# First FFN group's norm transposed on TensorE, its x tiles loaded together, mixer weight casts tied to the FFN's progress, weight ring in the gate/up region

## The chip, the cores and the metric

The kernel runs on all 8 cores of one Trainium2 chip. Each core takes two of the 16 sequences (4096 tokens) through the whole layer with its own copy of the weights; the cores exchange nothing. The time of a run is the device time of the slowest core in microseconds (us). Three runs of the kernel before gave 3274.52 to 3281.97 us, median 3280.74.

A core has five engines with one instruction queue each: TensorE (PE, matmuls; PEld is its weight load), VectorE (DVE), ScalarE (ACT), GpSimd (POOL) and SyncE (SP), which here issues DMAs only. An engine takes its queue in order, and an instruction that waits holds up all behind it. SP's and POOL's DMAs run on the same 16 DMA engines. SBUF (128 partitions) holds operands, PSUM has eight banks of 128x512 fp32 that matmuls write.

## The reference

One decoder layer, D = 1024, sequences of 2048:

```
x = x + 1/2 * SwiGLU_1(RMSNorm(x))                      # FFN1, d_ff = 2816
h = RMSNorm(x)
[q_lat | kv_lat | k_rope | xc | Bg | Cg | gate_logits] = h @ w_in
A: latent attention, 8 heads, QK-norm, rotary part, causal, softmax
B: y_B = Bg * conv3(Cg * xc)                            # causal depthwise, width 3
merged = sigmoid(gA) * (y_A @ w_proj_attn) + sigmoid(gB) * (y_B @ w_proj_conv)
x = x + merged @ w_out
x = x + 1/2 * SwiGLU_2(RMSNorm(x))                      # FFN2
swiglu(h) = (silu(h @ w_gate) * (h @ w_up)) @ w_down
```

x and the weights arrive as float32; the kernel's matmuls are bf16 with fp32 sums.

## The kernel before, in words

**Tiles and stages.** The 4096 tokens are 8 groups of 512 (NG, G), a group is four tiles of 128 (TPG). Three stages follow each other: FFN1 over all groups, the mixer (attention and convolution), FFN2. Sums between the stages go through DRAM (x1s, x2s). The FFN's inner width is 22 chunks of 128 (NFC).

**The norm** (`norm_stream`, L833) runs per tile: a load of x into one of two buffers (xin, L841), a square with a running sum on ACT (L860), two small POOL operations for 1/rms (L862, L864), one DVE operation that scales and rounds to bf16 (xn, L866), and a DMA transpose (L869) that writes hT, the group's activations with the features on the partitions. hT has two buffers for even and odd groups. The loads run one tile ahead.

**FFN1** (`ffn_stream`, L874): for each of 22 chunks, 8 matmuls for gate and 8 for up against hT (their issue is the helper's line L708), SiLU on ACT (L906), product on DVE (L908, aact). Then w_down. In the first group the loop over chunks kc is the outer one there, over all eight PSUM banks, so that it can follow the loading of w_down; x is added and stored to x1s (L937, L941).

**Weights.** FFN1's come as fp32 and are rounded on the core (`load_w1`, L779): gate/up pieces of 128x2048 through five staging buffers (astg, L783), rounded by ACT (L786) and DVE (L788) into agu; w_down in pieces of 128x1024 (L795) through four buffers (axr twice and dscr twice), rounded by ACT (L798) and DVE (L800) into awd. The weights of the mixer and of FFN2 are rounded from DRAM to DRAM (wms) by casting DMAs of POOL (`cast_w`, L820 and L830). `cast_w` waits for flags of FFN1's progress (`f1.1.0`, `f1.1.7`, ...), but a flag says that the planner has placed that work, not that the chip has done it.

**The ring.** In the mixer the convolution's, gate's and projections' weights pass through ten buffers of 128x1024 bf16 (`ring_stream`, L1186, in `use_order`). Its stream begins once FFN1 has been placed to its end.

**What sets the order.** Each stream above is a generator of operations. A planner (`FW.schedule`) takes at each step the operation with the earliest estimated start over all streams, with costs for each operation and rates for DMAs (DMA_RATE bytes per ns for SP, SWDMA_RATE for POOL), and appends it to its engine's queue with the semaphore waits that its buffers need. Among near equals the stream that stands first in the list goes first. So the order within every queue is fixed when the program is built; on the chip only the waits act.

**SBUF.** After the permanent buffers one region is laid out three times: for FFN1 (gate/up weights, sg, act, w_down, xr), for the mixer, and for FFN2. A buffer may be written once the work that used its addresses before has been placed, and the write waits on the chip for that work's semaphores. In the mixer's layout V and K of a whole sequence come one after the other, and the ring stands last, over FFN1's and FFN2's w_down and xr.

**The gated merge** (`proj`): per chunk of 128 features four products, gate A, gate B, conv (8 matmuls) and attention (4 matmuls), in three PSUM banks in turn; DVE reads the last two (L1319, L1321).

Of the kernel before, what the change touches and what calls it, by code (L numbers as in the profile page):

```python
# [177 lines left out]
class Op:  # L178
    __slots__ = ("eng", "fns", "reads", "writes", "cost", "sem", "nbytes")

    def __init__(self, eng, fns, reads, writes, cost, sem=None, nbytes=0):
# [6 lines left out]
        self.nbytes = nbytes  # L188

# [13 lines left out]
DMA_RATE = 340.0  # L203
# [3 lines left out]
class FW:  # L207
# [20 lines left out]
    def deps_of(self, op, commit):  # L228
# [17 lines left out]
        for group, is_w in ((op.reads, False), (op.writes, True)):  # L246
            for d in group:
# [220 lines left out]
def build_program():  # L468
# [19 lines left out]
    cst_d = nc.dram_tensor("cst", [128, 128], F32, kind="ExternalInput").ap()  # L488
# [81 lines left out]
    def ffn_bufs(tag):  # L570
# [30 lines left out]
    f1 = ffn_bufs("a")  # L601
    for b in f1.all:
# [14 lines left out]

    wlat = mb("wlat", [8, LATW], BF16)
# [13 lines left out]
    QT = [mb(f"QT{i}", [NH, G], BF16) for i in range(2)]  # L632
    d_QT = []
    for q_ in QT:
        dl = [Dep(f"QT.{t}") for t in range(TPG)]
        for dp in dl:
            dp.anc = list(q_.d[0].anc)
        q_.new = [(q_.addr, q_.end, dp) for dp in dl]
        q_.d = dl
        d_QT.append(dl)  # L640
    NKT = S // 128
    Vc = mb("Vc", [NKT, 4, 192], BF16, NKT)
    d_V = Vc.d
    NPT = 3
    KT = mb("KT", [NKT, NH, 128], BF16, NKT)
# [4 lines left out]
    M_END = a  # L650
# [46 lines left out]
    s_set = [fw.new_dma_sem(f"set{i}") for i in range(4)]  # L697
# [4 lines left out]
    def dma(eng, sem, fn, reads, writes, nbytes):  # L702
        return Op(eng, fn, reads, writes, 330.0 if eng == "sp" else 600.0, sem, nbytes)
# [73 lines left out]
    def load_w1():  # L777
        yield Wait(lambda: "seta" in flags)
        for c in range(NFC):  # L779
            yield Wait(lambda c=c: c < 2 or f"f1.t.0.{min(c - 2, TPG - 1)}" in flags)  # L780
# [8 lines left out]
                     [sb.d[1]], [gu.d[1]], c_dve(1024, 2))  # L789
        yield Do(lambda: flags.add("f1.stg"))  # L790
        yield Wait(lambda: "rope" in flags)
        for k in range(NFC):
# [19 lines left out]
    def cast_w():  # L812
        i = 0
        for n, F in mix_plan():
# [6 lines left out]
                      [], [d_wm[n]], 128 * F * 2)  # L821
# [12 lines left out]
    xc_ = {"xin": 0, "xr": 0, "xo": 0}  # L834

    def norm_stream(tag, src_d, srcdep, gi_, gate):
        def load(g, tt):
            i = xc_["xin"] % 2
            xc_["xin"] += 1
            r0 = g * G + tt * 128  # L840
            return i, dma("sp", s_xin[i], lambda e: e.dma_start(out=xin[i].t[:], in_=src_d[r0:r0 + 128, :]),  # L841
                          srcdep(g, tt), xin[i].d, 128 * D * 4)

        work = [(g, tt) for g in range(NG) for tt in range(TPG)]
        slots = {}
        nl = 0
        yield Wait(gate(0, "x"))
        yield ld_grow(gi_)
        for n, (g, tt) in enumerate(work):
            if tt == 0:  # L850
                yield Wait(gate(g, "h"))
            while nl < len(work) and nl <= n + 1:
                yield Wait(gate(work[nl][0], "x"))
                i, o_ = load(*work[nl])
                slots[nl] = i
                yield o_
                nl += 1
# [17 lines left out]
    def ffn_stream(tag, f, src_d, srcdep, dst_d, dstdep, bnk, start, xgate):  # L875
# [14 lines left out]
        for g in range(NG):  # L890
# [547 lines left out]
```

How the kernel before makes its waits and increments, by code:

```python
    def emit(self, op):  # L277
# [3 lines left out]
        waits = []  # L281
        for semk, val in deps.items():
            if eng.known.get(semk, 0) >= val:
                continue
            eng.known[semk] = val
            waits.append((self.sems[semk], val))
        fused = None
        if waits and op.eng != "pe":
            fused = waits.pop()
        for h, val in waits:
            eng.ops.append(lambda e, h=h, val=val: e.wait_ge(h, val))
        if op.sem is not None:
            eng.t = start + op.cost
            rate = SWDMA_RATE if op.eng == "pool" else DMA_RATE
# [11 lines left out]
            eng.count += 1  # L306
            h = self.sems[eng.sem]
            ev = (eng.count, eng.name, tf)
            key = eng.sem
            inc = 1
        n = len(op.fns)
        for i, fn in enumerate(op.fns):
            fw_ = fused if i == 0 else None
            if i == n - 1:
                if fw_ is not None:
                    eng.ops.append(lambda e, fn=fn, h=h, inc=inc, w=fw_: fn(e)._wait_ge(w[0], w[1]).then_inc(h, inc))
                else:
                    eng.ops.append(lambda e, fn=fn, h=h, inc=inc: fn(e).then_inc(h, inc))
            elif fw_ is not None:
                eng.ops.append(lambda e, fn=fn, w=fw_: fn(e)._wait_ge(w[0], w[1]))
            else:
                eng.ops.append(lambda e, fn=fn: fn(e))
        for d in op.writes:
# [84 lines left out]
    def final_wait(self, engname, semks):  # L408
# [3 lines left out]
            v = self.dma_vals[semk]  # L412
            if v > 0:
                eng.ops.append(lambda e, h=h, v=v: e.wait_ge(h, v))
```

## Time and profile before

| | us |
|---|---|
| median of 3 runs | 3280.74 |
| the profiled execution | 3284.44 |
| its span, first to last instruction, slowest core | 3282.9 |
| the eight cores' spans | 3255.2 to 3282.9 |
| PE busy | 3087.7 (94%) |
| DVE, ACT, POOL busy | 1137.6, 928.2, 669.6 |

The page's 40 slices of 82 us show where PE is not busy: 4, 8 and 6 tenths in the first three, then 9, with 7 and 8 where the mixer begins. The DMA engines are at 9, 9 and 6 tenths in the same three slices. Of the chain that ended last, PE is 83%, DMA 8%, all others 9%. A busy PE is not PE at its peak, since matmuls are pipelined and their ends are modelled.

The table of stretches and the timeline are to be read in us from the span's start. In a row of the timeline the brackets at the end tell how long the engine stood idle before it and what released it. PEclk is the granted clock as a share of 2.4 GHz; 0.50 is 1.2 GHz.

### The profile page before, as it was taken

How to read it: one execution, taken by the hardware profiler on the slowest of the kernel's cores; microseconds unless marked ns; L12 is line 12 of the kernel's file. 1: busy time of each engine (PE TensorE's matmuls, PEld its weight loads, DVE VectorE, ACT ScalarE, POOL GpSimd, SP SyncE). 2: the span in 40 equal slices, each digit the busy share in tenths (PEclk: the TensorE clock that was granted, in tenths of full speed). 3: DMA queues.
4: the chain of work that ended last, by engine and by line, in shares of the span. 5: the costliest groups of instructions: out<-in, count | busy, mean ns of one | idle time of the engine just before them, and what ended most of it. 6: DMA issues, size and time to landing. Idle time of an engine off the chain costs nothing.

```text
span 3282.9 us, 41375 instructions; the slowest of 8 cores (3255.2 to 3282.9 us)
## 1 busy us (share of the span) xinstructions
PE 3087.7 (94%) x14400; PEld 1407.1 (43%) x14400; DVE 1137.6 (35%) x1588; ACT 928.2 (28%) x1766; POOL 669.6 (20%) x1116
## 2 busy tenths in 40 slices
PE   4869999999997889999989999999999999999999
PEld 2324444444443344444434444444444444444444
DVE  4212212222233645363547463635221222222111
ACT  3311111111122453626433526364211111111100
POOL 0000000000014735352355453522100000000000
PEclk9989999999999999999999999999999999999999
DMA  9964256337426476575688685747761220221010
GB/s 288 280 132 81 68 90 111 68 70 131 103 68 143 95 187 155 148 185 148 173 178 203 160 193 152 188 128 214 226 191 50 90 71 22 88 90 46 33 52 26
DMA packets 337559, 420.34 MB, mean 128 GB/s; under 512 B 208976, under 2 KB 217296, under 8 KB 333776
## 3 DMA queue, kind: packets, MB, share of 16 engines
q1 hardware_dynamic: 329584, 381.88, 42.7%
q0 software_dynamic: 7776, 35.82, 9.0%
q8 instruction: 124, 2.03, 0.3%
q14 instruction: 75, 0.61, 0.1%
HBM read 355.38 MB, written 86.64 MB: 135 GB/s over the span
## 4 chain that ended last, share of the span: by engine, by line
PE 83%; DMA 8%; DVE 3%; POOL 2%; SPq 2%; issue 1%; ACT 1%; ACTq 0%; DVEq 0%; POOLq 0%
PE banks L708 83%; DMA axr_104<-ws 1%; DMA xin_69<-x1s 1%; SPq L869 1%; POOL hr L1063 1%; DMA xin_69<-x 1%; DMA KT<-kf 1%; DMA ring_136<-wms 1%; DVE Rs L1152 1%; POOL qf L1074 0%; DMA QT_120<-qf 0%; DVE T_108 L1039 0%; DMA astg_98<-ws 0%; DMA xo_131<-x1s 0%; DMA ring_134<-wms 0%
## 5 line engine op out<-in xcount | busy, mean ns | idle before, releaser
L708 PE MATMUL banks<-awd,aact 128*128 128x512 bf16 x1408 | 311.6, 383 | 32.0 <-ACT awd L798 22.4
L862 POOL TENSOR_SCALAR ssq<-ssq 128x1 f32<-128x1 f32 x96 | 20.5, 213 | 1523.5 <-ACT xn_70 L860 1431.3
L708 PE MATMUL banks<-cwd,cact 128*128 128x512 bf16 x1408 | 305.2, 379 | 0.0
L708 PEld LDWEIGHTS banks<-awd,aact 128*128 128x128 bf16 x1408 | 138.5, 99 | 202.5 <-issue 40.1
L708 PEld LDWEIGHTS banks<-cwd,cact 128*128 128x128 bf16 x1408 | 137.7, 98 | 166.2
L906 ACT ACTIVATE csg_166<-banks 128x512 f32<-128x512 f32 x88 | 52.5, 597 | 431.1 <-PE banks L708 431.1
L906 ACT ACTIVATE asg_94<-banks 128x512 f32<-128x512 f32 x88 | 52.5, 597 | 386.9 <-PE banks L708 385.6
L708 PE MATMUL banks<-QT_120,KT 128*128 128x512 bf16 (+3 forms) x384 | 134.6, 356 | 14.7 <-ACT pt_123 L1129 9.5
L908 DVE TENSOR_TENSOR cact<-csg_167,banks 128x512 bf16<-128x512 f32 x88 | 60.6, 688 | 246.0 <-PE banks L708 243.6
L908 DVE TENSOR_TENSOR cact<-csg_166,banks 128x512 bf16<-128x512 f32 x88 | 60.5, 688 | 239.5 <-PE banks L708 239.5
L908 DVE TENSOR_TENSOR aact<-asg_94,banks 128x512 bf16<-128x512 f32 x88 | 60.5, 688 | 237.7 <-PE banks L708 237.7
L1129 ACT ACTIVATE pt_123<-banks 128x512 bf16<-128x512 f32 (+2 forms) x216 | 115.9, 537 | 87.2 <-PE banks L708 85.0
L908 DVE TENSOR_TENSOR aact<-asg_95,banks 128x512 bf16<-128x512 f32 x88 | 60.5, 688 | 229.0 <-PE banks L708 229.0
L1129 ACT ACTIVATE pt_124<-banks 128x512 bf16<-128x512 f32 (+2 forms) x214 | 113.7, 531 | 60.4 <-PE banks L708 57.8
L1129 ACT ACTIVATE pt_125<-banks 128x512 bf16<-128x512 f32 (+3 forms) x210 | 110.2, 525 | 60.2 <-PE banks L708 54.9
L906 ACT ACTIVATE csg_167<-banks 128x512 f32<-128x512 f32 x88 | 52.5, 597 | 259.5 <-PE banks L708 259.5
L1152 DVE RECIPROCAL Rs<-Rs 128x128 f32<-128x128 f32 x128 | 121.4, 949 | 8.8 <-ACT Rs L1146 6.7
L906 ACT ACTIVATE asg_95<-banks 128x512 f32<-128x512 f32 x88 | 52.6, 597 | 238.4 <-PE banks L708 238.4
L1063 POOL TENSOR_TENSOR hr<-hm,nhalf 128x8 f32<-128x8 f32 x64 | 109.9, 1717 | 4.8
L708 PE MATMUL banks<-QT_119,KT 128*128 128x512 bf16 (+3 forms) x256 | 87.3, 349 | 17.1 <-DMA KT<-kf 11.9
L860 ACT ACTIVATE xn_70<-xin_68 128x1024 bf16<-128x1024 f32 x48 | 50.5, 1052 | 138.8 <-DMA xin_68<-x 54.3
L866 DVE SCALAR_TENSOR_TENSOR xn_71<-xin_69,rr,grow 128x1024 bf16<-128x1024 f32 x48 | 62.9, 1311 | 63.1 <-POOL rr L864 53.2
(433 smaller groups left out, 5492.2 us busy)
## 6 DMA issues: line engine op xcount, KB each, us to landing
wms<-ws POOLq DMA_DIRECT2D x33, 512.0 KB, 6.9
ring_134<-wms SPq DMA_DIRECT2D x52, 256.0 KB, 4.1
ring_136<-wms SPq DMA_DIRECT2D x51, 256.0 KB, 4.3
ring_138<-wms SPq DMA_DIRECT2D x51, 256.0 KB, 3.8
ring_140<-wms SPq DMA_DIRECT2D x51, 256.0 KB, 3.2
ring_142<-wms SPq DMA_DIRECT2D x51, 256.0 KB, 3.8
ring_135<-wms SPq DMA_DIRECT2D x39, 256.0 KB, 4.8
ring_137<-wms SPq DMA_DIRECT2D x39, 256.0 KB, 4.4
```

The source lines that it names most:

```text
L708: fns.append(lambda e, o_=o_, l_=l_, r_=r_, st=st, sp_=sp_: e.matmul(o_, lhsT=l_, rhs=r_, start=st, stop=sp_))
L860: yield op("act", lambda e, i=i: e.activation(out=xn[i].t[:], in_=xin[i].t[:], func=AF.Square, scale=1.0 / 32.0, accum_out=ssq.t[:, i, 0:1 ...
L862: yield op("pool", lambda e, i=i: e.tensor_scalar(out=ssq.t[:, i, 1:2], in0=ssq.t[:, i, 0:1], scalar1=EPS, scalar2=1.0, op0=ALU.add, op1=A ...
L866: yield op("dve", lambda e, i=i: e.scalar_tensor_tensor(out=xn[i].t[:], in0=xin[i].t[:], scalar=rr.t[:, i, 0:1], in1=grow.t[:], op0=ALU.mu ...
L869: yield dma("sp", s_tx[i], lambda e, i=i, h=h, tt=tt: e.dma_start_transpose(out=h.t[:, :, tt * 128:(tt + 1) * 128], in_=xn[i].t[:]), xn[i] ...
L906: yield op("act", lambda e, s_=s_, b0=b0: e.activation(out=s_.t[:], in_=bk(b0), func=AF.Silu), [d_bank[b0]], s_.d, c_act(512))
L908: pend = op("dve", lambda e, s_=s_, b1=b1, c=c: e.tensor_tensor(out=f.act.t[:, c, :], in0=s_.t[:], in1=bk(b1), op=ALU.mult), [s_.d, d_bank ...
L1063: yield op("pool", lambda e, jj=jj: e.tensor_tensor(out=hr.t[:, b, jj], in0=hm.t[:, b, jj], in1=nhalf.t[:, 0:8], op=ALU.pow), [hm.d[dj], n ...
L1129: yield op("act", lambda e: e.activation(out=p_.t[:, 0:w], in_=bk(b0)[:, 0:w], func=AF.Exp, scale=sc), [d_bank[b0]], p_.d, c_act(w))
L1152: yield op("dve", lambda e, qs=qs: e.reciprocal(out=R.t[:, qs], in_=R.t[:, qs]), R.d, R.d, 80 + 6.4 * 128)
```

## The change

**The first group's norm.** Its four x tiles are loaded at once, into the two xin buffers and the two xr buffers; the gains (grow) are loaded behind the first of them. Its transposes are done on TensorE: eight matmuls with an identity per tile into one PSUM bank (1 to 4), which one DVE copy takes to hT. All other groups keep the DMA transpose. The identity (identb) lies in the last block of act until then.

**The start.** `load_w1` no longer waits for the norm's flags (`f1.t.0.*`). `setup_b` with the rope tables stands behind `load_w1` in the list of streams. The matmuls of the first group are placed only behind the rounding of their weights (`f1.wg`, `f1.wd`); the w_down loads wait for `f1.n.0` too. DMA_RATE falls from 340 to 310.

**The casts.** An operation can have `after`: buffers whose last write it waits for on the chip. A mixer cast waits for the FFN1 product (act) of the chunk before its mark, or for the second sg buffer's last SiLU where the mark is a group's chunk 0, as it is for the first cast.

**The layout.** K and V are split by group (KT0, V0, ...). The first group's K and V and the ring now lie in FFN1's gate/up region, the rest behind. V's constant columns are set group by group.

**The merge.** The attention product comes before the conv product; the ring's order follows.

```diff
-DMA_RATE = 340.0
+DMA_RATE = 310.0
@@ deps_of
+        for d in op.after:
+            add(d.w, False)
@@ setup_a
+        yield dma("pool", s_set[4], lambda e: e.dma_start(out=identb.t[:], in_=cst_d[:, 128:256]), [], identb.d, 65536)
@@ load_w1
-            yield Wait(lambda c=c: c < 2 or f"f1.t.0.{min(c - 2, TPG - 1)}" in flags)
+            yield Do(lambda n_=f"f1.wg.{c}": flags.add(n_))
-        yield Wait(lambda: "rope" in flags)
+        yield Wait(lambda: "rope" in flags and "f1.n.0" in flags)
@@ cast_w
-                      [], [d_wm[n]], 128 * F * 2)
+                      [], [d_wm[n]], 128 * F * 2, [f1.act.d[at % 22 - 1]] if at % 22 else [f1.sg[1].d[0]])
@@ norm_stream
+        def xbuf(n):
+            if first and n in (2, 3):
+                ap, dd = f1.xr[n - 2]
+                return ap, dd, s_xr[n - 2]
+            return xin[n % 2].t[:], xin[n % 2].d, s_xin[n % 2]
-            while nl < len(work) and nl <= n + 1:
+            while nl < len(work) and nl <= (3 if first and n == 0 else n + 1):
+            if first and g == 0:
+                tb = 1 + tt
+                tv = banks[:, tb, :].bitcast(BF16).rearrange("p (a b) -> p a b", a=8)
+                yield Op("pe", [lambda e, k=k, i=i, tv=tv: e.transpose(out=tv[:, k, :], in_=xn[i].t[:, k * 128:(k + 1) * 128], identity=identb.t[:])
+                                for k in range(8)], [xn[i].d, identb.d], [d_bank[tb]], c_mm(128, 8))
+                yield op("dve", lambda e, hs_=hs_, tv=tv: e.tensor_copy(out=hs_, in_=tv), [d_bank[tb]], [d_hT[0][tt]], c_dve(1024, 2))
@@ mixer's layout
+    assert a <= R0 + NFC * 4096 - NRING * 2048
+    a = R0 + NFC * 4096 - NRING * 2048
+    ring = [mb(f"ring{i}", [1024], BF16) for i in range(NRING)]
@@ use_order
-            use_order += [(f"m4{c}", o_, F_) for o_, F_ in ((1536, 1024), (2560, 1024), (0, 1024), (1024, 512))]
+            use_order += [(f"m4{c}", o_, F_) for o_, F_ in ((1536, 1024), (2560, 1024), (1024, 512), (0, 1024))]
@@ streams
-        setup_b(),
         norm_stream("f1", x_d, lambda g, t: [], 0, gate1),
...
         load_w1(),
+        setup_b(),
```

What this does to the queues is shown at three places. Line numbers are each kernel's own, and the numbers behind names run on by one or more in the changed kernel: axr_103 and axr_104 before are axr_104 and axr_105 now, the ring's ring_134 to ring_143 are ring_126 to ring_135, FFN2's cgu_144 to cgu_165 are cgu_151 to cgu_172.

SyncE's queue at the program's start, before:

```order
L716 DMA par_sb<-par 128x312
L740 DMA dscr_65<-pos 128x32
L712 DMA grow<-rows 128x1024
L841 DMA xin_68<-x 128x1024
L841 DMA xin_69<-x 128x1024
L783 DMA astg_97<-ws 128x2048
L783 DMA astg_98<-ws 128x2048
L765 DMA css<-dscr_64 128x512
L869 DMA_TRANSPOSE hT_66<-xn_70 128x8x128
L841 DMA xin_68<-x 128x1024
L783 DMA astg_99<-ws 128x2048
L869 DMA_TRANSPOSE hT_66<-xn_71 128x8x128
```

The same place in the changed kernel:

```order
L747 DMA par_sb<-par 128x312
L883 DMA xin_68<-x 128x1024
L743 DMA grow<-rows 128x1024
L883 DMA xin_69<-x 128x1024
L883 DMA axr_104<-x 128x1024
L883 DMA axr_105<-x 128x1024
L814 DMA astg_98<-ws 128x2048
L814 DMA astg_99<-ws 128x2048
L814 DMA astg_100<-ws 128x2048
L814 DMA astg_101<-ws 128x2048
L814 DMA astg_102<-ws 128x2048
L772 DMA dscr_65<-pos 128x32
```

The four x tiles stand ahead of all weights, five weight loads follow without a transpose or a store between them, and no transpose into hT_66 is left for the first group.

GpSimd's queue where the first mixer casts stand, behind the norm of the third group's last tile, with the semaphores that each instruction waits for (e_act, e_dve: progress of ACT, DVE; e_pool: its own); before:

```order
L862 TENSOR_SCALAR ssq<-ssq 128x1 [waits e_act]
L864 TENSOR_TENSOR rr<-ssq,nhalf 128x1 [waits e_pool,e_dve]
L820 DMA wms<-ws 128x5632
L820 DMA wms<-ws 128x5120
L820 DMA wms<-ws 128x3072 x2
```

The same place in the changed kernel:

```order
L903 TENSOR_SCALAR ssq<-ssq 128x1 [waits e_act]
L905 TENSOR_TENSOR rr<-ssq,nhalf 128x1 [waits e_pool,e_dve]
L853 DMA wms<-ws 128x5632 [waits e_act]
L853 DMA wms<-ws 128x5120 [waits e_dve]
L853 DMA wms<-ws 128x3072 [waits e_dve] x2
```

The casts keep their place in the queue, behind twelve norms in both; each now has a wait of its own, the first for ScalarE, the others for VectorE.

SyncE's queue at the hand-over from mixer to FFN2, with ring loads between FFN2's gate/up pieces (cgu), before:

```order
L1186 DMA ring_143<-wms 128x1024
L809 DMA cgu_144<-wms 128x2048
...
L809 DMA cgu_153<-wms 128x2048
L1186 DMA ring_134<-wms 128x1024
L1186 DMA ring_135<-wms 128x1024
L809 DMA cgu_154<-wms 128x2048
```

The same place in the changed kernel:

```order
L1240 DMA ring_132<-wms 128x1024
L842 DMA cgu_151<-wms 128x2048
...
L842 DMA cgu_165<-wms 128x2048
L1240 DMA ring_133<-wms 128x1024
L1240 DMA ring_134<-wms 128x1024
L842 DMA cgu_166<-wms 128x2048
```

Ten pieces stood ahead of the first late ring load, fifteen do now. Of the 22 pieces two more follow near there, and the last five stand behind the mixer's last store, ahead of FFN2's w_down.

## Rows read from the trace of the kernel before

**Rows 1.** Stretches; us; busy us of PE, PEld, DVE, ACT, POOL; clock, DMA.

```profile
0.00:10.00 10.00, 0.00 (x0) 0.00 (x0) 3.96 (x8) 1.28 (x1) 1.10 (x6) 1.00 0.68 143
82.00:120.00 38.00, 38.00 (x178) 17.26 (x177) 14.81 (x23) 18.80 (x24) 0.00 (x0) 1.00 1.00 332
0.00:139.10 139.10, 95.63 (x430) 42.70 (x431) 55.52 (x81) 59.30 (x79) 11.71 (x30) 1.00 1.01 307
139.10:192.00 52.90, 21.80 (x85) 8.56 (x84) 2.70 (x4) 3.17 (x3) 2.16 (x5) 0.71 1.00 149
202.05:971.00 768.95, 768.95 (x3562) 348.85 (x3563) 177.92 (x238) 121.63 (x212) 37.42 (x73) 1.00 0.45 87
960.00:2400.00 1440.00, 1328.39 (x6298) 612.59 (x6297) 715.77 (x1016) 622.15 (x1268) 602.27 (x970) 0.97 0.68 169
```

**Rows 2.** Waits of TensorE from 0 to 210: for what, total us, times, longest.

```profile
PE banks L708 <- DMA hT_66<-xn_71: 42.6, 1, 42.6
PE banks L708 <- ACT awd L798: 22.4, 2, 12.0
```

**Rows 3.** Timeline and critical chain, first group's fourth x tile; start, us, what.

```profile
30.02 1.06 ACT L860 ACTIVATE xn_71<-xin_69 128x1024 bf16<-128x1024 f32 x1 [1.50 <-DMA xin_69<-x]
33.57 3.07 SPq L869 DMA_TRANSPOSE hT_66<-xn_71  x1
...
33.57 8.89 DMA hT_66<-xn_71
```

**Rows 4.** Timeline from 139 to 197, four engines.

```profile
139.13 2.14 POOL L820 DMA_DIRECT2D wms<-ws  x4
140.64 26.84 SPq L869 DMA_TRANSPOSE hT_66<-xn_71  x1
175.51 0.69 DVE L800 CAST awd<-dscr_65 128x1024 bf16<-128x1024 f32 x1 [33.51 <-DMA dscr_65<-ws]
191.93 5.19 PE L708 MATMUL banks<-awd,aact 128*128 128x512 bf16 x16 [12.00 <-ACT awd L798]
```

**Rows 5.** DMA view from 90 to 210: queues; then issues, us to landing.

```profile
q0 software_dynamic: 576, 4.33, 32.2%
...
wms<-ws POOLq DMA_DIRECT2D x1, 1408.0 KB, 21.9
```

**Rows 6.** Nearest rows to a transpose and its copy: timeline, then groups of instructions.

```profile
1071.65 0.22 PE L708 MATMUL banks<-QT_119,KT 128*128 128x128 bf16 x1
...
L1148 DVE COPY Xo<-banks 64x512 f32<-64x512 f32 x64 | 44.0, 688 | 93.9 <-PE banks L708 62.8 <-ACT Rs L1146 28.7 <-POOL pt_125 L1132 1.5
L1039 DVE TENSOR_TENSOR T_108<-banks,CQ 128x1024 f32<-128x1024 f32 x32 | 39.0, 1218 | 25.6 <-ACT SQ L1037 17.7 <-PE banks L708 7.1 <-POOL dscr_64 L1253 0.5
```

**Rows 7.** Timeline of TensorE, a chunk of gate/up in the first group.

```profile
48.89 3.62 PE L708 MATMUL banks<-hT_66,agu_73 128*128 128x512 bf16 x16
```

**Rows 8.** Timeline, SyncE's queue and TensorE at the start of the mixer.

```profile
1015.20 0.32 SPq L941 DMA_DIRECT2D x1s<-dscr_65  x1
1017.21 0.74 SPq L1186 DMA_DIRECT2D ring_134<-wms  x1
1028.35 1.86 PE L708 MATMUL banks<-hT_66,ring_134 128*128 128x512 bf16 x4 [9.09 <-DMA ring_134<-wms]
```

**Rows 9.** Timeline, SyncE's queue and TensorE at the hand-over to FFN2.

```profile
2272.94 0.38 SPq L809 DMA_DIRECT2D cgu_144<-wms  x1
2296.26 1.89 PE L708 MATMUL banks<-hT_67,ring_134 128*128 128x512 bf16 x8 [3.28 <-DMA ring_134<-wms]
```

**Rows 10.** Timeline, one chunk of the gated merge; then the reciprocal's group.

```profile
2322.84 1.89 PE L708 MATMUL banks<-convT,ring_138 128*128 128x512 bf16 x8
2324.56 1.03 PE L708 MATMUL banks<-attnT_129,ring_139 128*128 128x512 bf16 x4
2324.84 0.69 DVE L1319 SCALAR_TENSOR_TENSOR dscr_64<-dscr_64,banks 128x512 f32<-128x512 f32 x1 [1.11 <-PE banks L708]
...
L1152 DVE RECIPROCAL Rs<-Rs 128x128 f32<-128x128 f32 x128 | 121.4, 949 | 8.8 <-ACT Rs L1146 6.7
```

More of the change, by code:

```diff
@@ L178, with __init__ @@
 class Op:
-    __slots__ = ("eng", "fns", "reads", "writes", "cost", "sem", "nbytes")
-    def __init__(self, eng, fns, reads, writes, cost, sem=None, nbytes=0):
+    __slots__ = ("eng", "fns", "reads", "writes", "cost", "sem", "nbytes", "after")
+    def __init__(self, eng, fns, reads, writes, cost, sem=None, nbytes=0, after=()):
         self.eng = eng
@@ L188, in __init__ @@
         self.nbytes = nbytes
+        self.after = after
 def flat(lst):
@@ L580, in ffn_bufs @@
             a = f.sg[-1].end
+        if tag == "a":
+            f.ident = mk("identb", [128], BF16, a + (NFC - 1) * 1024)
+            f.ident.d[0].until = "f1.n.0"
+            commit_regs([f.ident])
         f.act = mk(f"{tag}act", [NFC, G], BF16, a, NFC)
@@ L631, in build_program, with q_buf, kv_bufs, KTt @@
     CQ = mb("CQ", [TPG, 128], F32)
-    QT = [mb(f"QT{i}", [NH, G], BF16) for i in range(2)]
-    d_QT = []
-    for q_ in QT:
+    def q_buf(i):
+        b = mb(f"QT{i}", [NH, G], BF16)
         dl = [Dep(f"QT.{t}") for t in range(TPG)]
         for dp in dl:
[L637 to L645, printed above, removed]
-    pt = [mb(f"pt{i}", [G], BF16) for i in range(NPT)]
+            dp.anc = list(b.d[0].anc)
+        b.new = [(b.addr, b.end, dp) for dp in dl]
+        b.d = dl
+        return b
+    KTg, Vg = [], []
+    def kv_bufs(i):
+        KTg.append(mb(f"KT{i}", [TPG, NH, 128], BF16, TPG))
+        Vg.append(mb(f"V{i}", [TPG, 4, 192], BF16, TPG))
+    QT = [q_buf(0)]
+    kv_bufs(0)
+    pt = [mb(f"pt{i}", [G], BF16) for i in range(NPT)]
+    assert a <= R0 + NFC * 4096 - NRING * 2048
+    a = R0 + NFC * 4096 - NRING * 2048
+    ring = [mb(f"ring{i}", [1024], BF16) for i in range(NRING)]
+    QT.append(q_buf(1))
+    d_QT = [b.d for b in QT]
+    for i in range(1, GPS):
+        kv_bufs(i)
+    def KTt(st):
+        return KTg[st // TPG].t[:, st % TPG]
+    def Vt(st):
+        return Vg[st // TPG].t[:, st % TPG]
+    d_KT = [d for b in KTg for d in b.d]
+    d_V = [d for b in Vg for d in b.d]
     Xo = mb("Xo", [G], F32)
@@ L653, in build_program @@
     mrgT = mb("mrgT", [8, G], BF16, 8)
-    NRING = 10
-    ring = [mb(f"ring{i}", [1024], BF16) for i in range(NRING)]
     assert a <= HI, (a, HI)
+    for b1_ in mall:
+        for b2_ in mall:
+            assert b1_ is b2_ or b1_.end <= b2_.addr or b2_.end <= b1_.addr
     for b in mall:
@@ L696, in build_program, with dma @@
     s_grow = fw.new_dma_sem("grow")
-    s_set = [fw.new_dma_sem(f"set{i}") for i in range(4)]
+    s_set = [fw.new_dma_sem(f"set{i}") for i in range(5)]
     def op(eng, fn, reads, writes, cost):
         return Op(eng, fn, reads, writes, cost)
-    def dma(eng, sem, fn, reads, writes, nbytes):
-        return Op(eng, fn, reads, writes, 330.0 if eng == "sp" else 600.0, sem, nbytes)
+    def dma(eng, sem, fn, reads, writes, nbytes, after=()):
+        return Op(eng, fn, reads, writes, 330.0 if eng == "sp" else 600.0, sem, nbytes, after)
     def mms(lst, reads, writes, n):
@@ L832, in cast_w, with load @@
         yield Do(lambda n_="f2.cast": flags.add(n_))
-    xc_ = {"xin": 0, "xr": 0, "xo": 0}
+    xc_ = {}
     def norm_stream(tag, src_d, srcdep, gi_, gate):
-        def load(g, tt):
-            i = xc_["xin"] % 2
-            xc_["xin"] += 1
+        work = [(g, tt) for g in range(NG) for tt in range(TPG)]
+        first = tag == "f1"
+        def xbuf(n):
[3 more added lines that the diff above has]
+            return xin[n % 2].t[:], xin[n % 2].d, s_xin[n % 2]
+        def load(n):
+            g, tt = work[n]
+            ap, dd, sem = xbuf(n)
             r0 = g * G + tt * 128
[L841 to L845, printed above, removed]
+            return dma("sp", sem, lambda e: e.dma_start(out=ap, in_=src_d[r0:r0 + 128, :]), srcdep(g, tt), dd, 128 * D * 4)
         nl = 0
         yield Wait(gate(0, "x"))
-        yield ld_grow(gi_)
+        if not first:
+            yield ld_grow(gi_)
         for n, (g, tt) in enumerate(work):
@@ L1303, in proj @@
                          [d_bank[b0], hgb.d], sx.d, c_act(512, 1))
-                b2 = nb()
+                b3 = nb()
                 yield rwait()
                 r = take(f"m4{c}")
-                for o_ in dense(b2, [(r.t[:, 128 * k:128 * k + 128], convT.t[:, k, :]) for k in range(8)], [r.d, convT.d]):
+                for o_ in dense(b3, [(r.t[:, 128 * k:128 * k + 128], aT.t[:, k, :]) for k in range(4)], [r.d, aT.d]):
                     yield o_
```

58 lines of the change are left out of this document (35 added, 23 removed).

## The prediction

> **What bounds the kernel now.** I read the table of stretches first. TensorE is busy for the whole of 202.05 to 971 and for 92% of 960 to 2400, but until 192 the DMA engines are what is full: a share of 1.01 up to 139.1 and 1.00 from there to 192, while TensorE works 95.63 us of the first 139.1 and 21.80 us of the next 52.9 [rows 1]. TensorE's waits in that part are 42.6 us for the transposed activations of the first group (hT) and 22.4 us in two waits for cast w_down pieces (awd) [rows 2]; the critical chain puts the last 8.89 us ahead of the first matmul on the DMA transpose of the group's fourth tile [rows 3].
>
> The second hole has another cause than the first. At 139.13 GpSimd sets off four weight casts (wms<-ws). From then on a transpose holds SyncE's queue for 26.84 us, a w_down cast on VectorE starts after 33.51 us without work, and the last w_down matmuls start only at 191.93 [rows 4]. The casts' queue took 32.2% of the DMA engines' time between 90 and 210 and moved 4.33 MB; the first cast, 1408 KB, landed after 21.9 us [rows 5]. So the first 202 us are bytes through the DMA engines in an order, and TensorE is fed by what comes out.
>
> **The front: what must be moved.** Until the last w_down piece has landed the changed kernel needs, by the tensors' sizes: 22 gate/up pieces of 1.05 MB and 22 w_down pieces of 0.52 MB (34.6 MB), 13 x tiles of 0.52 MB (three groups and one ahead, 6.8), the small tables and gains (1.5) and eight transposes of 0.26 MB instead of twelve (2.1): 45.1 MB. Before, 139.1 us at 307 GB/s are 42.7 MB [rows 1].
>
> - At the old pace the missing 2.4 MB at 332 GB/s take 7.2 us more: 146.3 us. That is the end on the dear side.
> - On the cheap side only the first 10 us are as slow as before (143 GB/s, 1.4 MB) and all the rest goes at the 332 GB/s of 82 to 120, a stretch without transposes [rows 1]: 10 + 43.7 / 0.332 = 141.6 us. Four transposes and the waits of SyncE between them are gone and twelve loads stand at the head of SyncE's queue without a wait, so I take 143, nearer to this end.
>
> The Trainium skill (DMA: Bandwidth & Descriptors, Specifications) gives about 358 GB/s as the share of one core in its HBM; the stretch shows 332, and by the page's figure the cheap end would be an estimate of 132 us. No stretch of 38 us here comes up to it, so I leave it to a rival.
>
> **The casts.** The hold doesn't reach the first cast. In GpSimd's order it stands where it stood, behind the twelfth norm, and what it waits for (the first group's last SiLU) has ended by then; only the second to fourth wait for VectorE's product of the second group. Price: in 139.1 to 192, 149 GB/s are 7.88 MB; without the casts' 4.33 MB, 3.55 MB are left, 10.7 us at 332 GB/s, so four casts cost 42.2 us, 9.7 us per MB, and the first (1.44 MB) 14.1 us [rows 1, 5]. Bounds: nothing, should it start behind the last w_down piece, and 21.9 us, its landing time [rows 5]. I take 14.1: the last piece lands at 143 + 14.1 = 157.1.
>
> The other three move into the second group's gate/up. Behind them in GpSimd's queue stand only the norms of the fourth group, due after that gate/up; beside them TensorE is busy for 768.95 of 768.95 us with a DMA share of 0.45 [rows 1], which hides them. Without that cover they would cost 42.2 - 14.1 = 28 us.
>
> From the last piece's landing (192) to the second group's first matmul (202.05) it was 10.1 us: a cast, 5.19 us of matmuls that begin on the lower clock [rows 4], and the residual loads. I keep it: 167.2 against 202.05, **34.9 us less**.
>
> **The transposes on TensorE.** Four times eight 128-wide matmuls. The trace has no transpose; the nearest row is a 128x128 matmul of 0.22 us, and twice that at half clock: 1.8 to 3.5 us for the last tile. The copy out of PSUM is bounded by 0.69 us (64x512 f32) and 1.22 us (128x1024 f32) [rows 6]. Together 2.5 to 4.7 us in place of 8.89 [rows 3]. The four tiles, no longer two at a time, have landed when 2.8 MB have moved: 10 us for 1.4 MB and 1.4 / 0.332 = 4.2 more, about 14; from a tile's first ScalarE row (30.02) to the transpose's issue (33.57) it is 3.6 us [rows 3], so the first matmul comes at 20 to 23 instead of 42.59. The Trainium skill (TensorE: Matmul & The Clock Gate, Part 4: PE-mode transpose) measures 275 to 390 ns for one in bf16, an estimate of 2.2 to 3.1 us for eight; the first matmul would still come at 20 to 23.
>
> These 20 us are not the gain. A chunk of 16 matmuls takes TensorE 3.62 us [rows 7], so 22 chunks of gate/up take 80 us and the 176 matmuls of w_down, eleven such chunks, 40: from 23 it could have all done at 143, and the last piece lands at 157. Starting early only lets TensorE wait inside the group for the same bytes. A chunk's weights take 1.05 MB / 0.332 = 3.2 us, close to those 3.62, so it is mostly the x tiles and transposes between them that slow it.
>
> **What I cost at nothing.** The rope tables behind the weight loads: VectorE is busy 55.52 of 139.1 us there [rows 1]; without that cover, as a wait for the scratch that w_down needs too, some us. The new DMA rate, a planner's number, moves nothing by itself. **The ring in the gate/up region:** in SyncE's queue the first ring load still stands right behind the last FFN1 store and a transpose. There that store goes out at 1015.20, the ring load at 1017.21, and its data end a wait of 9.09 us at 1028.35 [rows 8]: what held it was the queue, not the buffer. At the hand-over to FFN2 the last five gate/up pieces wait for the ring's region, so 17 instead of 22 stand about the ring loads; but 15 now stand ahead of the first late ring load where ten stood. Before, the pieces from 2272.94 on cost TensorE a wait of 3.28 us at a ring load [rows 9]. Five pieces are 5 x 0.52 / 0.332 = 8 us of queue, to be won or lost: -8 to +8, I take 0.
>
> **The exchanged projections.** Now the longer product (conv) is last and takes the bank that attention's took. VectorE reads each 0.28 us after its matmuls end, for 0.69 us (conv's eight matmuls make way at 2324.56, its read starts at 2324.84) [rows 10]. Both reads now follow conv: 0.28 + 0.69 + 0.69 + a hand-back of about 0.2 is 1.86 us against the 1.72 of the product between (2322.84 to 2324.56), 0.14 us late at 64 chunks, 9 us at most and nothing where attention's matmuls stand between. I take 1. The smaller V memsets, the split K and V and the rest of the replanned mixer: TensorE idles 111.6 us in 960 to 2400 [rows 1] in waits of a few us; a new order redeals them, -10 to +10, I take 0.
>
> **Sum.** -34.9 + 1 = -34 against the profiled execution, 3284.4 us: 3250. The median of the runs shown is 3.7 us under it: **3246**.
>
> **Rivals.**
> 1. *The cast is harmless, or the front faster.* For: the cast may be set off later than I place it, with most pieces landed; the 332 is a mean over 38 us and may be passed. Against: before, w_down pieces already issued when the casts began still landed late [rows 4]. Without the 14.1 us it is -34 - 14.1 = -48: 3232. The page's 358 speaks for this one.
> 2. *The queue stays the bound.* The cast starts earlier against the stream (about fifteen pieces issued instead of twenty), the transpose behind it again holds SyncE's queue, and the pieces behind that start late. For: the 26.84 us [rows 4]. With the landing's 21.9 in place of 14.1 and 146.3 in place of 143 it is -34 + 7.8 + 3.3 = -23, and with 7 us of the mixer against it -16: 3265.
> 3. *The exchange starves TensorE.* Where VectorE has a reciprocal of 0.95 us (949 ns) [rows 10] in front, each chunk is late by 0.14 + 0.95 = 1.09 us; at all 64, 70 us: -34.9 + 70 = +35: 3316. It decides against the change from 35 us on, half the chunks. Against: TensorE has attention in hand there and before there is no such wait [rows 10].
> 4. *The change doesn't do what it says:* the hold fails and all four casts go out together as before. Then the other three's 28 us come back: -34 + 28 = -6, 3275. Against: in the new order each of them waits for VectorE.
>
> **Chances.** The forecast 0.55 (3236 to 3258 by itself), rival 1 0.18, rival 2 0.15, rival 3 0.06, rival 4 0.06. The range of 3224 to 3268 takes in rivals 1 and 2 with the mixer's dealing and leaves the last two out. 0.2%, 6.6 us, is about what a measurement of this kernel can tell from no change: faster 0.88, same 0.06, slower 0.06.
>
> **What would show it.** A first gate/up matmul at 20 to 23 us; a DMA share near 1 up to about 157; one cast landing in the w_down stretch and w_down waits still there; the second group's first matmul near 167; a first ring wait near 9 us as before. I am wrong if that matmul comes before 155 or after 185, or if TensorE's idle time from there to FFN2 differs by over 12 us from before.

## The result and the profile after

The changed kernel takes 3230.35 us (median of all executions), the kernel before 3281.35 us in the runs beside it: a ratio of 0.9847 (95% interval 0.9820 to 0.9874), faster by 1.5%, some 51 us. The forecast was 3246, the range 3224 to 3268. The profiled execution takes 3227.39 us (span 3225.8, core 3), 57.05 less than the one of before. Executions in which the cores of a die ran at a lower clock are left out of all ratios here, and such dies out of all mean spans.

First the table of stretches, the columns as in [rows 1]; the first group ends at 154.2 now, and the second begins at 159.1.

```profile
0.00:10.00 10.00, 0.00 (x0) 0.00 (x0) 0.00 (x0) 2.43 (x3) 1.84 (x8) 1.00 0.68 135
0.00:159.10 159.10, 122.90 (x561) 54.41 (x562) 65.06 (x96) 61.69 (x82) 12.50 (x31) 0.99 0.99 301
112.00:154.20 42.20, 38.60 (x176) 16.95 (x176) 11.72 (x14) 13.06 (x16) 2.39 (x7) 1.00 1.01 309
159.10:940.00 780.90, 780.90 (x3617) 354.52 (x3618) 182.26 (x247) 126.15 (x223) 42.07 (x85) 1.00 0.39 94
930.00:2370.00 1440.00, 1343.35 (x6358) 616.55 (x6357) 712.82 (x1012) 623.65 (x1265) 599.10 (x964) 0.98 0.70 171
```

The stretch up to the second group, with the DMA engines full, ends at 159 in place of 202, at the old pace: 301 GB/s over 159 us against 307 over 139 [rows 1]. The stretch in which 149 GB/s moved [rows 1] is gone; in the w_down stretch it is 309, and TensorE works 38.60 of 42.20 us. The fourth and fifth rows answer to the last two of [rows 1]: TensorE is full while the casts run, and idles 96.65 us in the mixer's 1440 where it idled 111.61.

TensorE's waits from 25 to 160 (for what, total us, times, longest):

```profile
PE banks L739 <- DVE dscr_64 L989: 4.9, 1, 4.9
PE banks L739 <- ACT awd L830: 3.4, 2, 2.4
PE banks L739 <- ACT agu_90 L817: 2.6, 1, 2.6
```

The 22.4 us for cast w_down pieces [rows 2] are 3.4, a wait of 8.7 us in the kernel before for a piece that VectorE rounded is gone, and the first wait is for the residual's add, which was 4.9 in the kernel before too. The 42.6 us for the transposed tiles are replaced by the path below, the timeline of TensorE for the first group's fourth tile:

```profile
23.68 1.01 PE L914 MATMUL banks<-identb,xn_71 128*128 128x128 bf16 x8 [2.07 <-DVE xn_71 L907]
25.57 4.85 PE L739 MATMUL banks<-hT_66,agu_72 128*128 128x512 bf16 x11 [0.88 <-DVE hT_66 L916]
```

and of VectorE:

```profile
22.26 1.27 DVE L907 SCALAR_TENSOR_TENSOR xn_71<-axr_105,rr,grow 128x1024 bf16<-128x1024 f32 x1
24.73 0.69 DVE L916 COPY hT_66<-banks 128x1024 bf16<-128x1024 bf16 x1 [0.59 <-PE banks L914]
```

Eight transposes take 1.01 us and the copy 0.69, where the DMA transpose took 8.89 [rows 3]. The tiles' norms follow one another through two xn buffers, the last two 3.08 us apart (the third tile's transposes start at 20.60, the fourth's at 23.68). The first gate/up matmul at 25.57 is that of a late core; the mean of the eight is 23.1.

The timeline from 150 on shows the end of the first group and the first cast:

```profile
150.11 0.69 DVE L832 CAST awd<-axr_105 128x1024 bf16<-128x1024 f32 x1 [2.74 <-DMA axr_105<-ws]
159.10 6.06 PE L739 MATMUL banks<-hT_67,agu_72 128*128 128x512 bf16 x16 [4.88 <-DVE dscr_64 L989]
173.94 0.60 ACT L957 ACTIVATE asg_95<-banks 128x512 f32<-128x512 f32 x1 [2.85 <-PE banks L739]
174.84 0.59 POOL L853 DMA_DIRECT2D wms<-ws  x1 [43.12 <-ACT asg_95 L957]
```

The last w_down piece lands at 150.1 and the second group begins 9.0 us later. The first cast, which went out at 139.13 [rows 4], goes out at 174.84, released by ScalarE's SiLU of the second group's fourth chunk.

The start of the mixer and the hand-over to FFN2, answering to [rows 8, 9]:

```profile
971.73 0.32 SPq L993 DMA_DIRECT2D x1s<-dscr_65  x1
973.63 1.09 SPq L1240 DMA_DIRECT2D ring_126<-wms  x1
981.18 2.29 PE L739 MATMUL banks<-hT_66,ring_126 128*128 128x512 bf16 x5 [5.32 <-DMA ring_126<-wms]
...
2213.85 0.38 SPq L842 DMA_DIRECT2D cgu_151<-wms  x1
2220.71 1.87 PE L739 MATMUL banks<-hT_66,cgu_151 128*128 128x512 bf16 x4 [3.85 <-DMA cgu_151<-wms]
```

The ring load still leaves 1.9 us behind the last store (2.01 before [rows 8]), so the new place frees nothing there. The wait is 5.32 in place of 9.09, but that is a difference of the two cores: the mean of the eight is 5.4 us, and 5.6 before. At the hand-over one wait of 3.85 us at a gate/up piece stands where 3.28 stood at a ring load [rows 9].

### The profile page after: what moved, and what is told of

It is laid out like the page before. It is cut to its first block, busy times and chain, and to the rows that moved or that the text cites. A ratio compares the mean times of both kernels' runs of the same rounds, so it can differ in the third digit from the quotient of the medians.

```text
span 3225.8 us, 41313 instructions; the slowest of 8 cores (3201.6 to 3225.8 us)
## 1 busy us (share of the span) xinstructions
PE 3089.2 (96%) x14432; PEld 1406.9 (44%) x14432; DVE 1138.1 (35%) x1592; ACT 928.7 (29%) x1766; POOL 672.5 (21%) x1120
## 4 chain that ended last, share of the span: by engine, by line
PE 82%; DMA 7%; DVE 4%; POOL 4%; issue 2%; ACT 1%; SPq 1%; ACTq 0%; DVEq 0%; POOLq 0%
PE banks L739 82%; POOL hr L1117 1%; DMA xin_69<-x1s 1%; POOL qf L1128 1%; DMA axr_105<-ws 1%; DMA astg_101<-ws 1%; DVE Rs L1206 1%; DVE T_109 L1093 1%; DMA KT_141<-kf 0%; DMA QT_136<-qf 0%; DMA lt_0_115<-qk_0_113 0%; DVE hs L1095 0%; DMA cs_118<-css 0%; DMA xin_68<-x2s 0%; DMA xin_69<-x 0%
## 5 line engine op out<-in xcount | busy, mean ns | idle before, releaser
L903 POOL TENSOR_SCALAR ssq<-ssq 128x1 f32<-128x1 f32 x96 | 25.6, 267 | 945.2 <-ACT xn_70 L901 866.1
L853 POOL DMA_DIRECT2D wms<-ws x20 | 10.8, 538 | 564.1 <-DVE aact L959 521.0
L1202 DVE COPY Xo<-banks 64x512 f32<-64x512 f32 x64 | 44.0, 687 | 140.8 <-PE banks L739 78.6
```

Source lines behind the costliest of these rows:

```text
L903: yield op("pool", lambda e, i=i: e.tensor_scalar(out=ssq.t[:, i, 1:2], in0=ssq.t[:, i, 0:1], scalar1=EPS, scalar2=1.0, op0=ALU.add, op1=A ...
L1202: yield op("dve", lambda e: e.tensor_copy(out=X.t[po:po + 64, :], in_=bk(OB)[po:po + 64, :]), [d_bank[OB]], X.d, c_dve(512))
```

## The experiments

All differences below are read from marks in each kernel's profiled execution, as means over its eight cores, because they say where the time goes: the first gate/up matmul, the second group's first matmul, and the part from the mixer's first ring matmul to the first matmul of the last group's w_down in FFN2, which then fills TensorE without a break for the last 38 us in every kernel (the expectations call this mark the last matmul). From the second group's start to the first ring matmul every kernel takes 821.5 to 824.1 us. One execution stands behind the marks; beside them is the mean span of a core over all executions (24 spans and more), which tells how far a mark may be trusted. In the profiles of these kernels the tiles' names have no numbers.

| kernel | first gate/up | 2nd group | ring to last w_down | core's span | ratio to before (interval) |
|---|---|---|---|---|---|
| before | 40.5 | 199.9 | 2202.8 | 3262.1 | |
| changed | 23.1 | 157.1 | 2192.2 | 3212.5 | 0.9847 (0.9820 to 0.9874) |
| first_free | 22.7 | 173.0 | 2191.7 | 3232.7 | 0.9920 (0.9900 to 0.9941) |
| hold_only | 40.9 | 162.7 | 2200.0 | 3227.5 | 0.9923 (0.9873 to 0.9973) |
| no_hold | 23.4 | 199.4 | 2193.6 | 3258.1 | 0.9980 (0.9957 to 1.0003) |
| dma_tr | 52.6 | 174.4 | 2195.8 | 3241.7 | 0.9942 (0.9916 to 0.9967) |
| late_norm | 23.0 | 153.6 | 2191.4 | 3213.4 | 0.9820 (0.9770 to 0.9870) |
| ring_back | 22.7 | 159.1 | 2192.4 | 3220.4 | 0.9842 (0.9788 to 0.9896) |
| merge_back | 22.9 | 156.8 | 2192.6 | 3216.3 | 0.9821 (0.9765 to 0.9877) |
| rate340 | 22.9 | 156.8 | 2206.1 | 3228.9 | 0.9866 (0.9799 to 0.9933) |
| late2 | 23.0 | 151.1 | 2197.9 | 3215.3 | 0.9847 (0.9805 to 0.9890) |
| before_320 | 40.3 | 204.4 | 2189.4 | 3259.0 | 1.0007 (0.9990 to 1.0024) |
| rate325 | 22.9 | 158.2 | 2202.1 | 3222.8 | none formed |
| late2_300 | 23.0 | 152.9 | 2190.3 | 3207.8 | 0.9840 (0.9805 to 0.9874) |

### What the first cast costs

```diff
 first_free (against the changed kernel)
-  [f1.act.d[at % 22 - 1]] if at % 22 else [f1.sg[1].d[0]])
+  [f1.act.d[at % 22 - 1]] if at % 22 else [])
```

> The changed kernel with the wait of the first mixer cast (1408 KB) taken away; all queues keep their order. Bytes theory (the prediction's): this is the kernel that was predicted; the cast goes out behind the twelfth norm at about 131 us, takes 14.1 us of the stream, and the second group's first matmul comes at 159 + 14 = 173 us; the time is 3230 + 14 = 3244. Rival (harmless cast): by 131 most of w_down is in and TensorE has pieces in hand, first matmul 159 to 162 us, 3230 to 3233.

The second group begins 15.9 us later (157.1 to 173.0), 14.1 were priced. This kernel's timeline:

```profile
129.90 1.86 SPq L827 DMA_DIRECT2D axr<-ws  x2
132.26 0.59 POOL L853 DMA_DIRECT2D wms<-ws  x1
134.09 14.72 SPq L918 DMA_TRANSPOSE hT<-xn  x1
145.71 1.06 ACT L830 ACTIVATE awd<-axr 128x1024 bf16<-128x1024 f32 x1 [12.03 <-DMA axr<-ws]
146.91 3.57 PE L739 MATMUL banks<-awd,aact 128*128 128x512 bf16 x8 [7.79 <-ACT awd L830]
```

The cast goes out at 132.26; the next transpose holds SyncE's queue for 14.72 us, as the 26.84 of [rows 4] did behind four casts, and TensorE waits 7.79 us for a w_down piece. The price held, a harmless cast fell; over all executions the cores are 20.2 us longer (3232.7 against 3212.5).

The held queue alone does not explain the wait: the piece that TensorE waits for had been issued at 129.90, ahead of the cast and of that transpose, and was there only at 145.7; the one issued with it, at 153.6. The DMA queues from 125 to 175 us (packets, MB, share of the 16 engines' time):

```profile
q1 hardware_dynamic: 5884, 10.66, 70.4%
q0 software_dynamic: 144, 1.44, 24.3%
```

24.3% of 50 us are 12.2 us of all 16 engines for this cast, 8.4 us per MB, where the loads and transposes took 3.3; in the kernel before it was 8.9 per MB [rows 5]. The profile counts a cast by the bf16 that it writes; it reads twice those bytes. So an estimate of some 12 of the 15.9 us is the cast's own time on the engines; what the rest is, the runs don't show.

### The hold alone, and everything but the hold

```diff
 hold_only (against the kernel before): Op, dma and deps_of get `after`, and
-  [], [d_wm[n]], 128 * F * 2)
+  [], [d_wm[n]], 128 * F * 2, [f1.act.d[at % 22 - 1]] if at % 22 else [f1.sg[1].d[0]])
 no_hold (against the changed kernel): the same line the other way round
```

> The kernel before with the casts' holds alone (same marks); the first group keeps its DMA transposes. Bytes theory: without the casts 3.55 MB are left at 139.1 us, 10.7 us, so the last w_down piece lands at 150 and the second group's first matmul comes at 160 us as in the changed kernel: 3281 - 42 = 3239. Rival (TensorE sets the end): its first matmul stays at 42.6 us, 120 us of matmuls and some 9 us of waits end at 171 and the second group starts at 176: 3281 - 26 = 3255.

> The changed kernel without any hold of the casts. Bytes theory: four casts cost 42 us of the stream again, the second group's first matmul at about 201 us, 3230 + 42 = 3272, near the kernel before: all of the front's gain is the hold. Rival (TensorE sets the end, started 17 us earlier): w_down is further ahead of TensorE when the casts go out, so they cost 25 us, first matmul at 184, 3255.

hold_only: the second group at 162.7, 37.2 us earlier than before, near the bytes theory's 160 and far from 176. TensorE's timeline there:

```profile
41.95 78.76 PE L711 MATMUL banks<-hT,agu 128*128 128x512 bf16 x345 [41.95 <-DMA hT<-xn]
121.58 38.15 PE L711 MATMUL banks<-awd,aact 128*128 128x512 bf16 x173 [0.87 <-DVE aact L911]
164.05 11.19 PE L711 MATMUL banks<-hT,agu 128*128 128x512 bf16 x44 [4.32 <-DVE dscr L940]
```

Without the casts TensorE has no wait of a microsecond from its first matmul to the end of w_down, and the last w_down piece is there at 150.2 (mean of the cores), so here TensorE sets the end, as the rival had it, but sooner than its 120 us plus waits. no_hold: 199.4, where the kernel before has 199.9. All of the new front, its loads and TensorE's transposes, is worth 0.5 us as long as the four casts go out at 133:

```profile
133.12 2.13 POOL L853 DMA_DIRECT2D wms<-ws  x4
134.59 26.92 SPq L918 DMA_TRANSPOSE hT<-xn  x1
150.21 3.57 PE L739 MATMUL banks<-awd,aact 128*128 128x512 bf16 x8 [12.41 <-ACT awd L830]
```

### Transposes back on DMA

```diff
 dma_tr (against the changed kernel)
-            if first and g == 0:
+            if False:
                 tb = 1 + tt
```

> The changed kernel with the first group's transposes given back to DMA; its four x tiles are still loaded together, the casts still held. Bytes theory: four transposes of 0.26 MB are 3 us of stream, second group's first matmul at 162 us, 3233. Rival (TensorE sets the end): first gate/up matmul at 38 to 43 us in place of 25.6, second group's at 159 + 13 to 17 = 172 to 176, 3243 to 3247.

The second group comes 17.3 us later than in the changed kernel, so the bytes theory's 3 us fell. The rival's 172 to 176 came (174.4), its first matmul at 38 to 43 did not. SyncE's timeline shows where the time goes: with the x tiles loaded together and load_w1's wait for the norm gone, five weight pieces are on the way ahead of the first transposes.

```profile
10.68 18.76 SPq L918 DMA_TRANSPOSE hT<-xn  x2
35.01 9.24 SPq L918 DMA_TRANSPOSE hT<-xn  x1
46.25 3.78 SPq L918 DMA_TRANSPOSE hT<-xn  x1
```

Two transposes hold the queue for 18.76 us, a third for 9.24, and the first matmul comes at 52.6. From there to the second group it is 121.8 us, and 121.8 in hold_only too: TensorE's own length for a group, its closing wait included. That puts both theories into one rule, to which the section on the steps returns.

### The first group with fewer loads ahead

```diff
 late_norm (against the changed kernel), norm_stream and gate1
-  nl <= (3 if first and n == 0 else n + 1):
+  nl <= (3 if first and n == 0 else n if first and n == 7 else n + 1):
-            return lambda: "seta" in flags
+            return lambda: "seta" in flags and (g < 2 or "f1.wd.21" in flags)
 late2: n in (3, 7), and also (g < 1 or "f1.wg.21" in flags)
 late2_300: late2 with DMA_RATE = 300.0
```

> The changed kernel with the third group's x loads and transposes (four tiles, 3.15 MB with their transposes) put behind the last w_down load in SyncE's queue. If the bytes of the w_down stretch still end the first group, 3.15 MB at 300 GB/s are 10 us: the second group's first matmul would come at 147 us on the mean of the cores; but TensorE needs about 117 us from its first matmul (23.1) to the group's end, so 140 + 4.7 = 145 us is the floor: 145 to 149, time 3229 - 10 = 3219. Rival (the stream is paced by the four staging buffers and their rounding, not by bytes): 157 as now, 3229.

> The changed kernel with the second group's x loads and transposes behind the last gate/up load, and the third group's behind the last w_down load. If loads ahead of TensorE still cost the first group its waits (about 6 us on gate/up weights were left with the third group's tiles alone moved), the first group ends 117 to 120 us after its first matmul (23.1) and the second begins at 145 to 148 us, time 3218 to 3222. Rival (the transposes now stand in the w_down stream and hold SyncE there): w_down waits return, 154 to 160 us, 3227 to 3233.

late_norm begins the second group at 153.6, 3.5 us earlier, not 8 to 12: its w_down stretch has no wait left, but gate/up still waits for its weights (6.0 us in five waits on core 2). TensorE's timeline:

```profile
97.14 14.24 PE L739 MATMUL banks<-hT,agu 128*128 128x512 bf16 x63 [0.61 <-ACT agu L817]
112.33 38.15 PE L739 MATMUL banks<-awd,aact 128*128 128x512 bf16 x172 [0.94 <-DVE aact L959]
154.91 35.32 PE L739 MATMUL banks<-hT,agu 128*128 128x512 bf16 x147 [4.43 <-DVE dscr L989]
```

late2 reaches 151.1, 5.9 us earlier, and lost 5.7 in the mixer, whose order the planner dealt anew. Neither theory's number came; the transposes in the w_down stretch bring back waits of 0.50 and 2.76 us:

```profile
116.74 1.89 PE L739 MATMUL banks<-awd,aact 128*128 128x512 bf16 x8 [0.50 <-ACT awd L830]
121.39 24.29 PE L739 MATMUL banks<-awd,aact 128*128 128x512 bf16 x104 [2.76 <-DVE awd L832]
```

### Ring, merge and rate

```diff
 ring_back: ring made behind mrgT, no jump of `a`
 merge_back: the conv product and its ring piece ahead of attention's
 rate340, rate325 (changed kernel), before_320 (kernel before):
-DMA_RATE = 310.0
+DMA_RATE = 340.0    (325.0; 340.0 to 320.0)
```

> The changed kernel with the ring put last in the mixer's region again, over FFN1's w_down and xr (K and V stay split by group). The part from the mixer's first ring matmul to the last matmul is 2192.2 us now and was 2202.8 before (means of eight cores). Theory (the prediction's: the queue, not the buffer, holds the first ring load; re-dealing only): 2190 to 2196, first ring wait 5 to 9 us, 3225 to 3235. Rival (the ring's place is what the mixer gained): 2200 to 2204, 3240.

> The changed kernel with conv before attention again in the merge. Theory (the prediction's: the exchange costs about 1 us): from first ring matmul to the end 2191 us, 3228. Rival (the exchange is the mixer's gain, since attention's shorter product no longer stands between conv and its reader): 2200 to 2204, 3240.

> The changed kernel with the planner's DMA rate at 340 again. Theory (a planner's number moves nothing by itself): second group's first matmul at 157 us, the rest 2190 to 2196, 3229. Rival (the rate re-deals the mixer's queues and is where the 10.7 us came from): the rest 2198 to 2204, 3238.

By the marks the ring's place and the merge's order are worth nothing: 2192.4 and 2192.6 against 2192.2. Over all executions ring_back's cores are 7.9 us longer and merge_back's 3.8, and by time neither can be told from the changed kernel; a few us for the ring stay possible. By the marks the planner's rate alone gives all of the mixer's 10.7 us back, and 3 more (2206.1); over all executions the cores are 16.4 us longer. The waits of TensorE from 970 to 2420, changed kernel:

```profile
PE banks L739 <- DVE convT L1324: 12.2, 9, 2.5
PE banks L739 <- ACT pt_123 L1183: 10.3, 5, 3.3
PE banks L739 <- ACT pt_125 L1183: 2.2, 2, 2.1
PE banks L739 <- ACT pt_124 L1183: 2.0, 1, 2.0
PE banks L739 <- DMA ring_126<-wms: 5.3, 1, 5.3
```

and with 340:

```profile
PE banks L739 <- ACT pt L1183: 21.0, 10, 4.0
PE banks L739 <- DVE convT L1324: 18.5, 12, 3.0
PE banks L739 <- DMA ring<-wms: 10.4, 2, 8.6
```

The second list adds up the tiles of a name: softmax tiles (pt) 21.0 against 14.5, convT 18.5 against 12.2, the ring 10.4 against 5.3. The loss is spread over many short waits; only one of 8.6 for the ring stands out, and that is this core's (the mean of the eight is 5.8, 5.4 in the changed kernel).

> The kernel before with the planner's DMA rate at 320 in place of 340. Theory (the rate is a dealer: it gives the mixer a new order, good or bad by luck, not a better one as it falls): from the first ring matmul to the last matmul anything from 2192 to 2206 us, front unchanged at 199.9, time 3270 to 3284. Rival (a rate nearer to the 307 GB/s that the DMA engines give orders the mixer better): 2192 to 2197, 3272.

> The changed kernel with the planner's DMA rate at 325, between 310 (from first ring matmul to the last matmul 2192.2 us) and 340 (2206.1). Theory (a dealer): anywhere from 2190 to 2208, not on the line between the two. Rival (steady in the rate): 2198 to 2200, 3236.

> The changed kernel with the second group's norm behind the last gate/up load, the third group's behind the last w_down load, and the planner's DMA rate at 300; its front has the queues of the same kernel at 310 (second group's first matmul 151.1 us, from the first ring matmul to the last matmul 2197.9). Theory (a lower rate orders the mixer better, steadily): 2188 to 2193 there, second group's first matmul at 151, the last matmul at 3161 to 3166 on the mean of the cores, time 3216 to 3222, below the changed kernel's 3229. Rival (a dealer): 2194 to 2206, time 3224 to 3238.

325 gives 2202.1, above the line between its neighbours (2199.1), and 300 in late2 2190.3, inside its theory's range. 320 in the kernel before gives 2189.4 there, below both ranges expected, and loses 4.5 us in the front; its time isn't told from before (1.0007), and its cores' mean is only 3 us shorter, so its mark flatters it. So does no_hold's: 9.2 us below that of before, where its cores' mean is 4.0 us shorter. The execution behind the marks of before was 5 us longer than that kernel's mean, so 2202.8 may be some 5 us too long. Over all kernels, ten with 300 to 320 lie from 2189.4 to 2197.9, four with 325 and 340 from 2200.0 to 2206.1; with those 5 us taken off, before would lie at 2197.8 and the two sets would touch. In the changed kernel the rate is shown to matter (310, 325, 340: spans of 3212.5, 3222.8, 3228.9); that a lower rate is better in any kernel is not, and at one rate the order is still dealt (2191.4 to 2197.9 at 310). Which queue is ordered better, the runs don't show; it stays open.

late2_300 is the shortest by its cores' mean, 3207.8 against the changed kernel's 3212.5, and its executions go down to 3214.8 (the changed kernel's to 3226.1). Its ratio of 0.9840 and the changed kernel's 0.9847 have intervals that overlap, so by time the two are not told apart.

## Why the prediction was right, and where it was not

**The casts: the step that failed is "the hold doesn't reach the first cast".** The order listing shows for it only a wait on ScalarE, and I took the write that was last in the program's text, the first group's. The hold means the last write placed when the planner places the cast, and that was the second group's fourth SiLU (174.84). So the 14.1 us that the forecast kept were not paid. As a price they were right: 15.9 where the wait is taken away. first_free is the kernel that was predicted: 167.2 forecast, 173.0 measured on the mean.

**The stream: mis-sized.** I put the last piece at 143 without the cast, and 146.3 was the dear end; it lands at 150.1 on the profiled core, 148.0 on the mean. The bytes were right, 45.26 MB up to there against 45.1; the pace was not: 302 GB/s, and 313 without the first 10 us, where I took 332. On the profiled core the terms close: 167.2 - 14.1 (no cast) + 7.1 (stream) - 1.1 (a tail of 9.0, not 10.1) = 159.1, as measured: 42.95 us less, where 34.9 were forecast.

**The transposes: half right.** First matmul 25.6 (mean 23.1), forecast 20 to 23; 1.01 and 0.69 us for transposes and copy lie below my bounds of 1.8 and at the lower one of 0.69. "These 20 us are not the gain" is shown by no_hold (0.5 us), but only while the casts are in the way. The second group begins no sooner than the later of two: TensorE's first matmul plus 121.8, and the last piece plus about 9. The 121.8 us are measured twice, in hold_only and in dma_tr, 11.7 us apart in their start. With the hold alone the first is the later (40.9 + 121.8 = 162.7), with both the second (148.0 + 9 = 157.0, measured 157.1). So the hold by itself gives 37.2 of the 42.9, and the new front, on top of it, the last 5.6. The two are a floor, not the whole: in late_norm they give 144.8 and 150.9 (last piece at 141.9), measured 153.6, since waits inside gate/up push TensorE's own end back.

**Ring and hand-over:** 0 taken. ring_back's part from the ring's start to the end is 0.2 us off the changed kernel's, its front 2.0, its spans 7.9: the marks show no gain from the ring's place, the spans leave one of up to some 8 us open. **The exchange:** 1 us taken; merge_back is 0.4 us the other way, and of waits at the merge's reads (L1375) the changed kernel shows 1.8 us in 4. Rival 3 is out.

**The rate: the second step that failed, "moves nothing by itself".** It moves the planner's order, and with it 10 to 14 us of the mixer by the marks. The part behind the second group's start gained 14.1 us on the profiled cores and 11.0 on the means of the marks, past the -10 that I gave as the end. My sign for this, TensorE's idle time off by more than 12 us, came by the rows (96.65 against 111.61); on the mean of the cores it is 10 us, up to the last ring matmul (90.3 against 100.4).

**Sum.** -42.95 - 14.1 = -57.05 on the profiled executions, -34 forecast. The profiled execution of before was a long one: its cores' mean is 3267 us, 5 above their mean over all executions, which is why the medians differ by 51 and the means of the spans by 49.6; of the 14.1 some 7 are then left. Rival 1's 3232 is the nearest number, and its condition (a later cast) is what came; its front, 153.1, did not (159.1), and the rest of the likeness is the mixer's. Rival 4's price is measured by no_hold against first_free: the other three casts cost 26.4 us (199.4 against 173.0), 28 were given. Rival 2's held queue is seen in first_free, but the cast cost 15.9 us there, nearer to the 14.1 than to its 21.9.

The time is inside the range of 3224 to 3268 and outside the 3236 to 3258 that the forecast had by itself. The two failed steps gave 14.1 us each on the profiled executions and the stream took 7.1 back, so the number came in part by luck. Of the signs, the first gate/up matmul and the full DMA engines came; no cast landed in the w_down stretch, and the second group began at 159.1, not near 167.

## What to carry to other kernels

- Give a stage two clocks, the engine's start plus its own length and the last byte's landing plus the tail, and take the later as a floor: removing one cause is worth only the distance to the other (37.2 alone, 0.5 alone, 42.9 together).
- A wait built from "the last write so far" depends on when the planner places it. Find which write that is before pricing it.
- A number in a planner is an edit to every queue. Test it by itself; here, by the marks, it was worth as much as the whole gain of the mixer.

## What was not expected of the hardware

- One 1408 KB cast from DRAM to DRAM held a transpose in SyncE's queue for 14.72 us (first_free); four held one for 26.92 (no_hold). The first cost 15.9 us, where the 1.44 MB that it writes would be 4.7 us at the stretch's 309 GB/s and the 2.88 MB that it reads 9.3. The Trainium skill (DMA: Bandwidth & Descriptors, Queues, rings and completion order) has each DMA engine switch between queues packet by packet; no run shows the switching. What the runs show is the engines' time, 8.4 us per MB written by the cast beside 3.3 per MB of the other queue (first_free, 125 to 175), not why it is that much.
- DMA transposes behind five weight loads on the way held the queue for 18.76 us (two) and 9.24 us (one), against 3.07 [rows 3].
- Eight 128x128 bf16 transposes on TensorE took 1.01 us, at a granted clock of 1.00 (2.4 GHz) and after 2.07 us without work, and VectorE's copy of their 128x1024 bf16 out of PSUM 0.69 us, as long as a 64x512 copy of f32 [rows 6]. The Trainium skill (TensorE: Matmul & The Clock Gate, Part 4: PE-mode transpose) gives 275 to 390 ns for one; eight in a row took 126 ns each here.
